# RWKV chunk inverse: strict products moved to the opposite partition half, value products moved from level 1 to level 2

## The reference, cut to what matters

```python
def rwkv7_scan(r, w, k, v, a_, b_):
    def step(state, inp):
        r_t, w_t, k_t, v_t, a_t, b_t = inp
        sa = jnp.einsum('bhij,bhj->bhi', state, a_t)
        state = state * w_t[:, :, None, :] + sa[..., None] * b_t[:, :, None, :] + v_t[..., None] * k_t[:, :, None, :]
        return state, jnp.einsum('bhij,bhj->bhi', state, r_t)
```

## Time and profile before

| | us |
|---|---|
| median of 3 runs (lowest, highest) | 2909.98 (2908.98, 2912.18) |
| span of the profiled execution | 2902.5 |
| between that span and the median | 7.5 |
| TensorE busy | 2745.3 (95%) |
| VectorE busy | 1704.7 (59%) |
| eight head pairs, about | 1466 to 1998 of the span |
| one pair, from one to the next | 65.45 |

### The profile page before, as it was taken

The page is one execution under the profiler, slowest core; times in us unless marked ns, Lnnn a source line. Parts: engine busy times, 40 slices in busy tenths (PEclk is TensorE's granted clock), DMA queues, the critical chain, the costliest instruction groups (busy, mean ns, idle before and its releaser), DMA issues.

```text
span 2902.5 us, 42598 instructions
## 1 busy us (share of the span) xinstructions
PE 2745.3 (95%) x17241; PEld 2000.0 (69%) x17241; DVE 1704.7 (59%) x2286; ACT 649.1 (22%) x1091; POOL 185.8 (6%) x203
## 2 busy tenths in 40 slices
PE   5899798999999999999989999998979999999998
PEld 3455455888878878888555565674557788788887
DVE  7688786555457665554455666553355585655554
ACT  4133422111010121110222332321341111211102
POOL 2000111000000000000120001110000010100001
PEclk8999899999999999999999999998999999999999
DMA  7476402333333323333201111111113333233332
GB/s 242 125 234 202 119 23 73 94 94 92 96 87 94 94 86 95 88 97 98 76 22 44 40 33 33 33 55 48 49 36 89 91 107 102 82 88 95 99 96 72
DMA packets 393991, 255.47 MB, mean 88 GB/s; under 512 B 19880, under 2 KB 376833, under 8 KB 393729
## 3 DMA queue, kind: packets, MB, share of 16 engines
q1 hardware_dynamic: 390256, 243.63, 28.6%
q0 software_dynamic: 2320, 5.11, 0.6%
q10 hardware_dynamic: 1280, 4.78, 0.4%
HBM read 250.60 MB, written 2.10 MB: 87 GB/s over the span
## 4 chain that ended last, share of the span: by engine, by line
PE 79%; DVE 5%; issue 2%; ACT 1%; POOL 1%; DVEq 0%; POOLq 0%; ACTq 0%
PE PS L832 14%; PE PS L831 14%; PE PS L833 14%; PE PS L1580 4%; PE PS L1555 3%; PE PS L846 3%; PE PS L847 3%; PE PS L848 3%; PE PS L1646 2%; PE PS L1672 1%; PE PS L1561 1%; PE PS L1670 1%; PE PS L1765 1%; PE PS L1446 1%; PE PS L1787 1%
## 5 line engine op out<-in xcount | busy, mean ns | idle before, releaser
L857 DVE CAST WH<-W 128x1024 fp32r<-128x1024 f32 x304 | 213.5, 702 | 417.8 <-PE PS L833 372.3
L832 PE MATMUL PS<-XNL,WH 128*128 128x512 f32 x960 | 381.9, 398 | 0.0
L859 DVE TENSOR_TENSOR WL<-W,WH 128x1024 fp32r<-128x1024 f32 x304 | 374.6, 1232 | 10.4
L831 PE MATMUL PS<-HH,WH 128*128 128x512 f32 x672 | 262.0, 390 | 0.1
L833 PE MATMUL PS<-HH,WL 128*128 128x512 f32 x672 | 261.5, 389 | 0.0
L832 PE MATMUL PS<-HL,WH 128*128 128x512 f32 x672 | 261.5, 389 | 0.0
L832 PEld LDWEIGHTS PS<-XNL,WH 128*128 128x128 f32 x960 | 180.9, 188 | 41.6 <-issue 0.5
L833 PE MATMUL PS<-XNH,WL 128*128 128x512 f32 x512 | 201.7, 394 | 0.0
L831 PE MATMUL PS<-XNH,WH 128*128 128x512 f32 x512 | 201.2, 393 | 0.0
L831 PE MATMUL PS<-XN2H,WH 128*128 128x512 f32 x448 | 178.5, 398 | 10.6 <-issue 6.7
L833 PE MATMUL PS<-XN2H,WL 128*128 128x512 f32 x448 | 177.7, 397 | 0.0
(11 more groups left out here) (501 smaller groups left out, 4709.1 us busy)
## 6 DMA issues: line engine op xcount, KB each, us to landing
ARENA<-in_ada_w SPq DMA_DIRECT2D x80, 512.0 KB, 5.2
W<-in_ffn_w SPq DMA_DIRECT2D x64, 512.0 KB, 4.0
W<-in_w_in SPq DMA_DIRECT2D x51, 512.0 KB, 4.3
W<-in_ffn_w_gate SPq DMA_DIRECT2D x44, 512.0 KB, 3.8
W<-in_ffn_w_up SPq DMA_DIRECT2D x44, 512.0 KB, 3.8
W<-in_ffn_w_down SPq DMA_DIRECT2D x32, 512.0 KB, 4.0
W<-in_sc_w_in SPq DMA_DIRECT2D x24, 512.0 KB, 3.8
W<-in_ada_w SPq DMA_DIRECT2D x16, 512.0 KB, 4.8
```

Source lines behind the costliest of these rows:

```text
L831: nc.tensor.matmul(dst, WH[:, h, c], hi(k), start=(start and k == 0), stop=False)
L832: nc.tensor.matmul(dst, WH[:, h, c], lo(k), start=False, stop=False)
L857: nc.vector.tensor_copy(WH[:, h, :], W[:, s, 0:D]).then_inc(parted, 1)
L859: nc.vector.tensor_tensor(WL[:, h, :], W[:, s, 0:D], WH[:, h, :], ALU.subtract).then_inc(freed[s], 1)
```

## The change

Where a chunk's own half is c, the other half is called far.

- Gram g: its 16 wide products with the first key operand (64x128) are cut in two of 64x64: the strict one is now written to the far half, the row one to the own half. The 16 with the second operand stay (64x128, own half).
- ab: X's gram goes to the far half; 16 more products make Z's gram in the own half, into columns of the same two banks. VectorE's za reads it from PSUM instead of GR, and the wait for g3 ahead of xa is gone.
- MT and X so lie in the far half, Z in the own half. p reads far and writes own. xz makes X from Z and PM (own half) into the far half, and Z into the own half. X products of head e go to bank 2+2e, Z products to bank 3+2e (before, both to bank 2+e). z adds read two banks.
- The akv products move from behind xz of level 0 into p of level 1, one beside each p product; ScalarE's copy of them moves from behind pm of level 0 to behind pm of level 1. They count to the steps p10 and p11.

```diff
@@ -539,10 +539,10 @@
...
                + " ".join(f"p{l}0 p{l}1" + (next_pair("kss") if l == 3 else " bonus " if l == 4 else " ") + f"xz{l}0 xz{l}1"
-                          + (" akv" if l == 0 else "") for l in levels)
+                          for l in levels)
...
 steps["act"] = (("raw0" if ahead else "dila") + " tr0 tr1 tr2 tr3 "
-                + " ".join(f"pm{l}0 pm{l}1" + (next_pair("raw1") + "akv" if l == 0 else next_pair("ksq") if l == 1
+                + " ".join(f"pm{l}0 pm{l}1" + (next_pair("raw1") if l == 0 else " akv" + next_pair("ksq") if l == 1
@@ -1618,13 +1618,19 @@
...
             pe.wait_ge(p_act.sem, p_act.done("tr0", at))
-        for w in range(2):
+        for part in ("strict", "rows", "keys"):
...
                     cols = slice(t * P + c * CHUNK, t * P + (c + 1) * CHUNK)
-                    at_col = (t % 2) * 4 * CHUNK + w * 2 * CHUNK
-                    dst = bank[(4, 5, 6, 0)[2 * (t // 2) + e]][own, at_col:at_col + 2 * CHUNK]
-                    mm = nc.tensor.matmul(dst.rearrange("p (w t) -> p w t", w=2), BKT[h, w, cols], AR[h, t, :, own], start=True, stop=True)
+                    at_col = (t % 2) * 4 * CHUNK + ("strict", "rows", "keys").index(part) * CHUNK
+                    gram = bank[(4, 5, 6, 0)[2 * (t // 2) + e]]
+                    if part == "strict":
+                        mm = nc.tensor.matmul(gram[halves[1 - c], at_col:at_col + CHUNK], BKT[h, 0, cols], AR[h, t, 0, own], start=True, stop=True)
+                    elif part == "rows":
+                        mm = nc.tensor.matmul(gram[own, at_col:at_col + CHUNK], BKT[h, 0, cols], AR[h, t, 1, own], start=True, stop=True)
+                    else:
+                        dst = gram[own, at_col:at_col + 2 * CHUNK].rearrange("p (w t) -> p w t", w=2)
+                        mm = nc.tensor.matmul(dst, BKT[h, 1, cols], AR[h, t, :, own], start=True, stop=True)
@@ -1632,7 +1638,11 @@
...
                 cols = slice(t * P + c * CHUNK, t * P + (c + 1) * CHUNK)
-                mm = nc.tensor.matmul(bank[1 + e][own, t * CHUNK:(t + 1) * CHUNK], AR[h, t, 0, own], BKT[h, 0, cols], start=True, stop=True)
+                nc.tensor.matmul(bank[1 + e][halves[1 - c], t * CHUNK:(t + 1) * CHUNK], AR[h, t, 0, own], BKT[h, 0, cols], start=True, stop=True)
+        for e, h in enumerate(halves):
+            for c, own in enumerate(halves):
+                cols = slice(t * P + c * CHUNK, t * P + (c + 1) * CHUNK)
+                mm = nc.tensor.matmul(bank[1 + e][own, (NT + t) * CHUNK:(NT + t + 1) * CHUNK], BKT[h, 0, cols], AR[h, t, 0, own], start=True, stop=True)
@@ -1642,8 +1652,12 @@
...
             for t in range(NT):
-                for own in halves:
-                    mm = nc.tensor.matmul(bank[e][own, t * CHUNK:(t + 1) * CHUNK], MT[own, 4 * e + t, :], XZ[own, e, 0, t, :], start=True, stop=True)
+                n = 4 * e + t
+                for c, own in enumerate(halves):
+                    far = halves[1 - c]
+                    mm = nc.tensor.matmul(bank[e][own, t * CHUNK:(t + 1) * CHUNK], MT[far, n, :], XZ[far, e, 0, t, :], start=True, stop=True)
+                    if l == 1:
+                        mm = nc.tensor.matmul(bank[6][own, n * HEAD:(n + 1) * HEAD], GR[own, n, 2, :], TOK[own, t, 3, halves[e]], start=True, stop=True)
@@ -1665,19 +1679,14 @@
...
                 n, cols = 4 * e + t, slice(t * CHUNK, (t + 1) * CHUNK)
+                for c, own in enumerate(halves):
+                    if l < len(LEVELS) - 1:
+                        nc.tensor.matmul(bank[2 + 2 * e][halves[1 - c], cols], XZ[own, e, 1, t, :], PM[own, n, :], start=True, stop=True)
                 for own in halves:
-                    if l < len(LEVELS) - 1:
-                        nc.tensor.matmul(bank[2 + e][own, cols], XZ[own, e, 1, t, :], PM[own, n, :], start=True, stop=True)
-                for own in halves:
-                    mm = nc.tensor.matmul(bank[2 + e][own, NT * CHUNK + t * CHUNK:][:, 0:CHUNK], PM[own, n, :], XZ[own, e, 1, t, :], start=True, stop=True)
+                    mm = nc.tensor.matmul(bank[3 + 2 * e][own, cols], PM[own, n, :], XZ[own, e, 1, t, :], start=True, stop=True)
...
             early(range(2 * l - 1, 2 * l))
-        if l == 0:
-            for n, (e, t) in enumerate(items):
-                for own in halves:
-                    mm = nc.tensor.matmul(bank[6][own, n * HEAD:(n + 1) * HEAD], GR[own, n, 2, :], TOK[own, t, 3, halves[e]], start=True, stop=True)
-            mm.then_inc(p_pe.sem, p_pe.step("akv"))
@@ -2278,10 +2287,10 @@
...
             nc.scalar.activation(PM[:, 4 * e:4 * e + 4, :].rearrange("p n t -> p (n t)"), bank[e][:, 0:NT * CHUNK], ACT.Copy).then_inc(p_act.sem, p_act.step(f"pm{l}{e}"))
-        if l == 0:
-            if ahead:
-                raw("rw", 1, i, 7, p_act)
-            act.wait_ge(p_pe.sem, p_pe.done("akv", at))
+        if l == 0 and ahead:
+            raw("rw", 1, i, 7, p_act)
+        if l == 1:
+            act.wait_ge(p_pe.sem, p_pe.done("p11", at))
@@ -2953,9 +2962,8 @@
...
     dve.wait_ge(p_pe.sem, p_pe.done("ab", at))
-    dve.wait_ge(p_dve.sem, p_dve.done("g3", at))
     tt(xs, PS[:, 1:3, 0:NT * CHUNK].rearrange("p e (t d) -> p e t d", t=NT), both("level1_t"), ALU.mult).then_inc(p_dve.sem, p_dve.step("xa"))
-    tt(zs, GR[:, :, 0, :].rearrange("p (e t) d -> p e t d", e=2), both("level1"), ALU.mult).then_inc(p_dve.sem, p_dve.step("za"))
+    tt(zs, PS[:, 1:3, NT * CHUNK:2 * NT * CHUNK].rearrange("p e (t d) -> p e t d", t=NT), both("level1"), ALU.mult).then_inc(p_dve.sem, p_dve.step("za"))
@@ -2964,9 +2972,9 @@
...
             dve.wait_ge(p_dve.sem, p_dve.done(f"z{l - 1}{e}" if l else "zi", at))
-            new = slice(0 if l < len(LEVELS) - 1 else NT * CHUNK, 2 * NT * CHUNK)
-            own = XZ[:, e, :, :, :].rearrange("p w t d -> p (w t d)")[:, new]
-            tt(own, own, bank[2 + e][:, new], ALU.add).then_inc(p_dve.sem, p_dve.step(f"z{l}{e}"))
+            first = 0 if l < len(LEVELS) - 1 else 1
+            own = XZ[:, e, first:2, :, :].rearrange("p w t d -> p w (t d)")
+            tt(own, own, PS[:, 2 + 2 * e + first:4 + 2 * e, 0:NT * CHUNK], ALU.add).then_inc(p_dve.sem, p_dve.step(f"z{l}{e}"))
...

```

## The result

| | before | changed |
|---|---|---|
| median of the runs, us (lowest, highest) | 2911.08 (2908.98, 2913.76) | 2879.04 (2875.17, 2880.49) |
| ratio, 95% interval | | 0.9891 (0.9878, 0.9905) |
| span of the profiled execution | 2902.5 | 2873.4 |
| of it: up to the first pair's first transpose | 1466.65 | 1468.63 |
| the mixer, from there to the last chunk state product | 515.89 | 485.08 |

Four executions of the kernel before stand behind 2911.08 us, where the three ahead of the prediction had 2909.98. The last four rows are worked out from the starts of TensorE's records in the two traces. The stretch before the mixer took 2.0 us longer in the changed kernel's profiled execution, and nothing in it was changed; the mixer itself is 30.8 us shorter. The time forecast was 2879.2 us, the sum for the mixer 30.8 us.

A forecast was written before the change was run, and what follows sets the result against it. TensorE's own issue was taken to bound the levels. Six middle pairs at 3.71 us, the first at 4.0 and the last at 4.5 save 30.8 us: span 2871.7 plus 7.5 gives 2879.2 us, range 2872 to 2892.

The forecast's parts named there:

- xz of levels 1 to 3: X and Z products in four quarters take 0.93 us instead of 1.87 per level, gaining 2.79 us a pair.
- Level 0: From xz to the filler behind p of level 1: 2.83 us instead of 3.88, 1.05 gained; some 0.8 becomes a wait.
- akv beside p: In p of level 1, akv and p share four quarters in p's own 0.93 us, so akv costs nothing.
- Grams: Extra products cost TensorE 0.06 us in g and 0.47 in ab; 0.40 is covered, +0.13 us a pair remains.
- The g3 wait: Without this wait VectorE's xa starts 0.60 us behind the mask, not 0.71: -0.11 us, useful only in first and last pair.
- First and last pair: Grams are hidden behind idle time in both; gains of 4.0 us in the first pair and 4.5 in the last.
- Sum: Six middle pairs at 3.71 us give 22.3 us; with the first and last pair 30.8 us in total.
- From span to median: Whole kernel: span 2902.5 - 30.8 = 2871.7 us, plus 7.5 us between span and median, gives 2879.2 us.
- A: New orders in xz and p with akv don't pack: 3 us slower, 2913 us, no change; chance 0.08.
- B: VectorE's z chain takes over in every level: 6 to 13 us paid, 2885 to 2892 us; chance 0.13.
- C: Each turn between own and opposite placement in xz and p drains the array: 41 us slower, 2951 us; chance 0.04.

The follow-up runs named there:

- the delays on VectorE: Changed kernel with extra VectorE operations ahead of z of head 0 in levels 2 and 3: 0.17 us gave median 2881.23 us, 0.66 us gave 2889.85 us.
- the order-only kernel: Kernel before with only akv interleaved with p of level 1 and its copy moved, all placed in the own half: 2913.88 us, ratio 1.0018.

## Why the prediction was right, by its own steps

- *xz of levels 1 to 3*: forecast 2.79 us a pair, measured 2.76: from xz to its filler 2.01 - 1.09 = 0.92 each (changed kernel, level 3):

```profile
1564.90 0.28 PE L1684 MATMUL PS<-ARENA 64*64 64x64 f32 x2
...
1565.99 1.12 PE L1580 MATMUL PS<-HXF,W 128*128 128x512 f32 x2
1567.05 1.15 PE L1658 MATMUL PS<-ARENA 64*64 64x64 f32 x32
```

 Packing in four quarters holds for X and Z of one half together, and TensorE stays the path, with 0.33 us of slack (0.36 forecast). Shown by the delays on VectorE.
- *Level 0*: forecast 1.05, measured 3.88 - 2.91 = 0.97. The wait is there: xz's last record starts at 1552.45 and p's first at 1553.20, 0.75 us later (0.7 to 0.8 forecast), of which the profile counts 0.52 as idle. p10 starts 1.69 us after xz (1.66 forecast), p11's first record 2.28 (2.26). The rest of the miss of 0.08 lies in p11 with its akv products, which begin anew behind a wait: 0.62 us from their first record to the filler, 0.57 forecast. VectorE's part of level 1 wasn't late after all: the operation that took 1.19 us in the earlier trace rows took 0.90, so z of level 1 ran at its due time.
- *akv beside p*: it costs nothing there, as forecast. What the forecast didn't say, though its own sum held it, is that the move gains nothing either: with akv left behind xz a middle pair is as long. The whole gain there is from the placement of X and Z (with Z in a bank of its own). Placement without the move: all of it. The move without placement: 0.27 us lost.
- *Grams*: forecast +0.13 us a pair, measured +0.13 (9.23 for 9.10). The filler behind ab starts 0.53 us later in the pair, as forecast (4.74 for 4.21), and 0.40 of it is covered. Taking the Z gram away gives 0.28 of its 0.47 us back, so the cover by xi is as it was reckoned.
- *The g3 wait*: forecast 0.11 us, in the last pair alone; measured 0.20 there, by one execution.
- *First and last pair*: forecast 4.0 and 4.5. Up to the next pair's start the first is 4.20 us shorter; the last, up to its first chunk state, 4.61. In the first, p of level 0 comes 0.44 us earlier (15.15 to 14.71, and 14.70 to 14.74 in all executions with the new placement), where 0.16 was put in; the rest is 3.76 (3.84). In the last it is 0.21 (0.11) for p of level 0, 1.64 (1.6) for level 0, 2.76 (2.79) for levels 1 to 3. What the clock moves there is as large as these misses: in the changed kernel's profile p and xz of level 0 of the last pair run at 0.54 and p of level 1 at 1.00,

```profile
1918.70:1922.40 3.70, 3.60 (x96) 3.48 (x96) 1.16 (x2) 0.77 (x2) 1.27 (x2) 0.54 0.58 221
1922.40:1924.20 1.80, 1.57 (x65) 1.29 (x65) 0.69 (x1) 0.38 (x1) 0.64 (x1) 1.00 0.00 0
```

 while the last pair's first chunk state comes at 38.56 us there and at 38.1 to 38.9 us in the other executions whose levels in that pair are meant to be the same.
- *Sum*: a middle pair 3.60 us, forecast 3.71; in all 30.8 us in the mixer, forecast 30.8. That the two agree to the digit is luck of small misses of both signs: 0.11 x 6 too much in the middle pairs, 0.3 too little in the first and last, and 0.34 us more behind the last pair's first chunk state that nothing was forecast for.
- *From span to median*: 2871.7 + 7.5 = 2879.2 us were forecast, 2873.4 + 5.6 = 2879.0 measured. The span came out 1.7 us longer (the stretch ahead of the mixer took 2.0 more), the other term 1.9 us shorter. That the two cancel is luck too. The term is no property of the kernel: each of the changed kernel's executions is only 1.8 to 3.0 us longer than its own span, and the rest is the difference between the profiled execution and the middle one.
- *Rivals*: A (no packing) is what the order-only kernel shows, at 29 ns a record and 0.27 us a pair lost (0.38 forecast for the change, gram cost included). It is wrong for the change. B (the z chain takes over) is true at level 0, where the forecast had it, and not elsewhere. C (a turn between placements drains the array) is refuted: the change turns between own and far within every four products, at 14.6 ns a record. The floor of about 25 ns of the Trainium skill's page "TensorE: Matmul & The Clock Gate", section "Wait — 56ns, not 53.3ns?", doesn't hold for neighbours in different quarters: 64 records started within 0.94 us.

Not tried was X and Z in one PSUM bank again with the far placement, so whether the second bank is needed stays open. That a second bank alone doesn't halve the time is seen in the order-only kernel.

## What to carry to other kernels

Where small products of one kind fill only the diagonal quarters of the TensorE array, look for a second, equally frequent kind that can be placed in the other two: here keeping one of two recursively updated matrices in the opposite partition half halves the issue time at the cost of one more gram. Interleave them so that each four neighbours have four quarters: grouped by eight, 0.41 of the 0.93 us that an xz gains were lost, while the two orders tried within four came out the same. Before moving work off the path, ask what it covered: akv hid VectorE's additions, and moving it away gained nothing until something else (a filler) took its place.

## What was unexpected of the hardware

TensorE starts products ahead of others that were issued before them, when those go to other quarters of the array: with X and Z grouped by eight, Z's first records start (1560.54) while six X records are outstanding, and p's first records start (1556.41) while six of akv's are. The reach was three products in both cases, worth 0.17 us at a turn of the grouped xz. It is narrow enough that an order by eight loses 1.47 us a pair against the order by two, and wide enough that a turn between two streams is partly free. The starts show this; the ends of these records are modelled.
